# Retention by heads in a two-layer decoder step: half units of weights, 32-row state updates in four row groups

## What is computed

```python
RET_HEADS = 4; RET_QK_DIM = 256; RET_V_DIM = 512
q, k, v, g = jnp.split(x @ w_in, [hq, 2 * hq, 2 * hq + hv], axis=-1)    # w_in: 1024 x 6144
q, k = rope(q, pos), rope(k, pos) * RET_QK_DIM ** -0.5
inner = jnp.einsum('bihd,bjhd->bhij', q, k) * dmask[None]
o = jnp.einsum('bhij,bjhv->bihv', inner, v) + \
    jnp.einsum('bihd,bhdv->bihv', q, state) * cross_decay[None, :, :, None]
new_state = chunk_decay[None, :, None, None] * state + \
    jnp.einsum('bjhd,bjhv->bhdv', k * k_decay[None, :, :, None], v)
on = ((of - mu) * lax.rsqrt(var + LN_EPS)) * gain
return (jax.nn.silu(g) * on) @ w_out                                    # w_out: 2048 x 1024
```

## Time and profile before

| what | value |
|---|---|
| time, median of 3 runs (lowest to highest) | 1177.4 us (1176.07 to 1180.37) |
| profiled execution, span | 1174.3 us, mean granted clock 0.974 |
| TensorE products busy | 1087.4 us, 93% |
| VectorE busy | 569.8 us, 49% |
| ScalarE busy | 329.5 us, 28% |
| DMA | 319.72 MB, mean 272 GB/s |
| retention with its output products | 548.3 to 896 us |
| experts of layer 1 | 896 to 1174.3 us |
| share of the chain that ended last | TensorE 76%, DMA 9%, VectorE 9% |

### The profile page before, as it was taken

One profiled execution on the slowest core, in us unless ns is written; L12 is line 12 of the kernel. 1 busy time (PEld: TensorE's weight loads), 2 busy tenths in 40 slices (PEclk: granted clock), 3 DMA queues, 4 the chain that ended last, 5 costly groups with the idle time before them and its releaser, 6 DMA issues.

```text
span 1174.3 us, 14472 instructions
## 1 busy us (share of the span) xinstructions
PE 1087.4 (93%) x5486; PEld 638.7 (54%) x5486; DVE 569.8 (49%) x1080; ACT 329.5 (28%) x532; POOL 42.6 (4%) x77
## 2 busy tenths in 40 slices
PE   6999988999999899988999999999799899998991
PEld 5877655645443434335888765456687443434330
DVE  3877585636232223229684336658547323232325
ACT  4335256404111111113444213326413211111110
POOL 1300000000000000000000001111000000000000
PEclk9999999989999999999999999999898999999996
DMA  9434381946599999991433468996538699999951
GB/s 315 123 122 155 115 318 55 380 172 258 213 428 428 429 428 428 412 370 43 143 126 117 145 222 306 355 338 254 176 147 323 250 429 428 428 429 428 411 201 45
DMA packets 62842, 319.72 MB, mean 272 GB/s; under 512 B 4978, under 2 KB 5010, under 8 KB 50370
## 3 DMA queue, kind: packets, MB, share of 16 engines
q1 hardware_dynamic: 54338, 288.93, 62.2%
q0 software_dynamic: 8160, 28.80, 6.6%
q10 hardware_dynamic: 288, 1.23, 0.3%
HBM read 296.05 MB, written 22.89 MB: 272 GB/s over the span
## 4 chain that ended last, share of the span: by engine, by line
PE 76%; DMA 9%; DVE 9%; ACT 2%; issue 2%; SPq 1%; DVEq 0%; POOL 0%; ACTq 0%; POOLq 0%
PE bank L1147 27%; PE bank L979 17%; PE bank L1008 7%; DMA ring<-in_w_exp_up 7%; PE bank L946 3%; PE bank L1436 3%; PE bank L1212 2%; DMA ring<-in_w_in_attn 1%; PE bank L958 1%; PE bank L1426 1%; PE bank L959 1%; PE bank L1451 1%; PE bank L1308 1%; PE bank L1344 1%; PE bank L1330 1%
## 5 line engine op out<-in xcount | busy, mean ns | idle before, releaser
L1147 PE MATMUL bank<-ring_parts,XTt_parts 128*128 128x512 f32 x576 | 182.7, 398 | 4.0 <-DVE ring_parts L2153 2.8
L1147 PE MATMUL bank<-ring_parts 128*128 128x512 f32 x576 | 181.4, 393 | 0.0
L979 PE MATMUL bank<-ring,XTt 128*64 128x512 f32 x768 | 169.5, 598 | 11.8 <-DMA ring<-in_w_exp_up 9.9
L1147 PEld LDWEIGHTS bank<-ring_parts,XTt_parts 128*128 128x128 f32 x576 | 107.2, 190 | 33.2 <-issue 10.9
L979 PEld LDWEIGHTS bank<-ring,XTt 128*64 128x64 f32 x768 | 56.9, 138 | 121.3 <-issue 105.5
L1147 PEld LDWEIGHTS bank<-ring_parts 128*128 128x128 f32 x576 | 107.9, 189 | 24.4 <-issue 1.8
L1976 DVE TENSOR_TENSOR arena<-XTt,bank 128x512 f32<-128x512 f32 x16 | 17.2, 1073 | 208.9 <-PE bank L979 208.9
L1008 PE MATMUL bank<-ring,arena 128*64 128x512 f32 x512 | 115.1, 602 | 0.0
L694 DVE TENSOR_TENSOR ring_parts<-ring,ring_parts 128x4096 fp32r<-128x4096 f32 x22 | 97.1, 4419 | 33.6 <-ACT ring_parts L689 33.6
L689 ACT ACTIVATE ring_parts<-ring 128x4096 fp32r<-128x4096 f32 (+1 forms) x26 | 83.6, 3224 | 15.3 <-DMA ring<-in_w_in_attn 7.1
L1600 ACT ACTIVATE arena<-bank 128x512 f32<-128x512 f32 (+6 forms) x116 | 53.5, 489 | 93.6 <-PE bank L1147 48.9
(11 more groups left out here) (258 smaller groups left out, 1267.3 us busy)
## 6 DMA issues: line engine op xcount, KB each, us to landing
ring<-in_w_exp_down SPq DMA_DIRECT2D x32, 2048.0 KB, 13.4
ring<-in_w_exp_up SPq DMA_DIRECT2D x32, 2048.0 KB, 16.5
ring<-in_w_exp_gate SPq DMA_DIRECT2D x16, 2048.0 KB, 12.2
arena<-in_w_exp_gate SPq DMA_DIRECT2D x16, 2048.0 KB, 18.1
ring<-in_w_in_ret SPq DMA_DIRECT2D x12, 2048.0 KB, 9.0
ring<-in_state_ret SPq DMA_DIRECT2D x16, 1024.0 KB, 6.6
out_state_s<-ring POOLq DMA_DIRECT2D x16, 1024.0 KB, 6.3
ring<-in_w_in_attn SPq DMA_DIRECT2D x6, 2048.0 KB, 8.2
```

The costliest lines, as they stand in the source:

```text
L979: last = pe.matmul(ps[64 * j:64 * j + 64, :], xs[:, k, x0:x0 + 64], w[:, k, :], start=(k == 0), stop=(k == KC - 1))
L1147: last = pe.matmul(ps[:, 0:width], x(t, a, k), w[c][:, k, 0:width], **at)
```

## The change

Retention is written anew as six rounds. Round p has the units 2p and 2p + 1 of a new order of `w_in`: unit 2h is q and k of head h side by side (256 columns of each), unit 2h + 1 its v, units 8 to 11 the gates. In rounds 1 to 4 TensorE makes, between the tiles of these units, all of head p - 1: scores, the sample's outputs from its states, the prompt's state and outputs, and the updates of the head's sample states. Every unit is loaded, copied, split and multiplied in two halves of four lines (1 MB): raw halves in slots 0 and 5, copies in slot 4. The head's sample states are four pieces (two sequences each, 1 MB) in slots 1 and 2; each is updated, stored, and reloaded with the next head's. An update is four products of 32 rows. The roped tiles of q and k alternate between the two buffers of `RR` in all rounds; ScalarE copies the keys out (`keys_of`) and applies the prompt's key decay, which was VectorE's (L2387). The sample's moments go with the prompt's, head by head. The output units 0 to 3 get slots 1, 0, 5, 1 and copies in 2, 3, 4, 2. The order of the first expert loads is as it was.

The diff, cut to its core:

```diff
-          + [("rin", u) for u in range(8)] + [("state", 0), ("rin", 8), ("state", 1), ("rin", 9), ("state", 2)]
...
+          + [("retention", 0)] + [("rout", u) for u in range(4)]
...
-    for n, where, copy_at in ((0, 0, 2), (1, 1, 3), (2, 5, 4), (3, 0, 2)):
+    held[0], held[1], held[2] = ("rin", 10), ("pieces", 0), ("pieces", 1)
+    held[3] = held[4] = held[5] = ("rin", 11)
+    for n, where, copy_at in ((0, 1, 2), (1, 0, 3), (2, 5, 4), (3, 1, 2)):
...
+    def update(h, r):
+        for i in range(4):
+            take(("update", h, r, i), 4 + i)
...
+        def high_half(act, j):
+            act.wait_ge(half_in[j % 4], HALF_LANDED[j])
+            if j < 2:
+                wait_let_go(act, ("moe0", 3 * NE - 2))
+            else:
+                half_done(act, j - 2)
+            act.activation(unit_high()[:, half_lines(j)], unit_raw(j // 2)[:, half_lines(j)], ACT.Copy).then_inc(half_high, 1)
```

The loads, on the SP queue:

```diff
+            for p in range(5):
+                half(4 * p + 4)
+                half(4 * p + 5)
+                if 1 <= p < RH:
+                    piece(p, 0)
+                    piece(p, 1)
+                half(4 * p + 6)
+                if 1 <= p < RH:
+                    piece(p, 2)
+                half(4 * p + 7)
+                if 1 <= p < RH:
+                    piece(p, 3)
```

The update products and the order of a round, on TensorE:

```diff
+            def update(h, r):
+                if r == 0:
+                    pe.wait_ge(twice_ready, h + 1)
+                    pe.wait_ge(k_copied, 3 * h + 3)
+                pe.wait_ge(kd_ready, 4 * h + r + 1)
+                for i in range(4):
+                    ps, c, own = fill(("update", h, r, i)), i // 2, slice(32 * i, 32 * i + 32)
+                    pe.matmul(ps[:, :], kd[own, r % 2, c * 128:(c + 1) * 128], v[own, 2, h, :], start=True, stop=True)
...
+            for p in range(6):
+                a, b, h = 2 * p, 2 * p + 1, p - 1
+                works = 0 <= h < RH
+                if p == 0:
+                    first_half()
+                else:
+                    part_of(a, 0, 0)
+                    if works:
+                        scores_of(h)
+                    part_of(a, 0, 1)
+                    if works:
+                        sample_out(h)
+                        states_of(h)
+                    else:
+                        turn_o(a - 9, 0)
+                    part_of(a, 0, 2)
+                    if works:
+                        outputs_of(h)
+                part_of(a, 1, 0)
+                if works:
+                    update(h, 0)
+                elif p:
+                    turn_o(a - 9, 1)
+                part_of(a, 1, 1)
+                part_of(a, 1, 2)
+                if works:
+                    update(h, 1)
+                elif p:
+                    turn_o(a - 9, 2)
+                turn, n = (turn_qk, p) if p < RH else (turn_o, b - 9)
+                part_of(b, 0, 0)
+                part_of(b, 0, 1)
+                turn(n, 0)
+                if works:
+                    update(h, 2)
+                part_of(b, 0, 2)
+                part_of(b, 1, 0)
+                turn(n, 1)
+                part_of(b, 1, 1)
+                if works:
+                    update(h, 3)
+                part_of(b, 1, 2)
+                turn(n, 2)
```

Rope, sums and the order of rounds 0 to 3 and of the start of round 4, on VectorE:

```diff
+            def rope_qk(h, t):
+                k, r = 3 * h + t, ROWS[t]
+                if t == 2:
+                    fold(NIN + 2 * h + 1, ("rin", 2 * h, t), RE[:, k % 2, :])
...
+                if k >= 2:
+                    wait_full(dve, "rturn", (k - 2) // 3, (k - 2) % 3)
+                    dve.wait_ge(k_copied, k - 1)
+                rope(RE[:, k % 2, :], RR[:, k % 2, :], rropeA, table_r[:, t], 2, RQ, r, (re_used, k + 1), rk_ready)
...
+            def updated(h, r):
+                for i in range(4):
+                    ps = wait_full(dve, "update", h, r, i)
+                    st = pieces[r][:, i % 2, i // 2, :]
+                    dve.scalar_tensor_tensor(out=st, in0=st, scalar=GAMMA8[h], in1=ps[:, :],
+                                             op0=ALU.mult, op1=ALU.add).then_inc(freed(("update", h, r, i)), 1)
...
+                if p < RH:
+                    if works:
+                        scales(h)
+                    rope_qk(p, 0)
+                    if works:
+                        updated(h, 0)
+                        keys_for(h, 2)
+                    rope_qk(p, 1)
+                    rope_qk(p, 2)
+                    if works:
+                        updated(h, 1)
+                        keys_for(h, 3)
+                    low_half(dve, 2 * a + 3)
+                    if works:
+                        updated(h, 2)
+                    low_half(dve, 2 * a + 4)
+                    if works:
+                        updated(h, 3)
+                    fold(NIN + a + 2, ("rin", a + 1, 2), v[:, 2, p, :])
+                elif works:
+                    scales(h)
+                    gate(0, 0)
+                    updated(h, 0)
+                    keys_for(h, 2)
+                    gate(0, 1)
+                    half(0)
+                    updated(h, 1)
```

More of the change, by code:

```diff
@@ L100 @@
 PLACE, BEFORE, HIGH, HIGH_BEFORE = plan_slots()
[L101 removed]
+PARTED = [("in", u) for u in IN_ORDER] + [("rout", n) for n in range(4)]
 WIDE = 256 + 2 * SAMPLE
@@ L644, in wait_let_go @@
         def wait_let_go(eng, key):
-            if key and key[0] == "state":
-                for half in range(2):
-                    eng.wait_ge(state_stored[key[1]][half], 16)
+            if key and key[0] == "pieces":
+                for r in (2 * key[1], 2 * key[1] + 1):
+                    eng.wait_ge(piece_stored[r], 32 * RH)
             elif key and key[0] == "rout" and key[1] % 2 == 0:
@@ new lines, in first_half @@
+            def first_half():
+                pe.wait_ge(half_high, 1)
+                for t in range(3):
+                    wait_emptied(pe, "x2", t, 0)
+                    wait_emptied(pe, "x2", t, 1)
+                    project(fill(("rin", 0, t)), t, x_parts, unit_parts(0), stop=False, of=(0,), ks=range(4))
+                pe.wait_ge(half_low, 1)
+                for t in range(3):
+                    last = project(bank[t], t, x_parts, unit_parts(0), start=False, stop=False, of=(1,), ks=range(4))
+                last.then_inc(half_used, 1)
@@ L1465, in turn_o, with turn_qk @@
+            def turn_qk(h, t):
+                k, r = 3 * h + t, ROWS[t]
+                pe.wait_ge(rk_ready, k + 1)
+                ps = fill(("rturn", h, t))
+                for c in range(4):
+                    last = pe.transpose(ps[:, c * 128:c * 128 + r], RR[0:r, k % 2, c * 128:(c + 1) * 128], ident[0:r, 0:r])
+                last.then_inc(full(("rturn", h, t)), 1)
             def turn_o(n, t):
@@ new lines, in sample_out @@
+            def sample_out(h):
+                wait_emptied(pe, "sinner", h)
+                wait_emptied(pe, "rin", 2 * h + 1, 2)
+                pe.wait_ge(qm_ready, h + 1)
+                ps = fill(("so", h))
+                for g in range(2):
+                    pe.matmul(ps[32 * g:32 * g + 32, :], innS[0:64, 32 * g:32 * g + 32], v[0:64, 2, h, :], start=True, stop=False)
+                for r in range(4):
+                    pe.wait_ge(piece_in[r], 32 * (h + 1))
+                    for c in range(2):
+                        for g in range(2):
+                            at = 64 * c + 32 * g
+                            last = pe.matmul(ps[at:at + 32, :], QM[:, c, 4 * g + r, :], pieces[r][:, g, c, :],
+                                             start=(c == 1 and r == 0), stop=(r == 3))
+                last.then_inc(full(("so", h)), 1)
@@ L2416, in state @@
-            def state(s):
-                st = weights(("state", s))
-                for j in range(8):
-                    h, c, _ = update_of(j)
-                    ps = wait_full(dve, "update", s, j)
-                    dve.scalar_tensor_tensor(out=st[:, 2 * h + c, :], in0=st[:, 2 * h + c, :], scalar=GAMMA8[h], in1=ps[:, :],
-                                             op0=ALU.mult, op1=ALU.add).then_inc(freed(("update", s, j)), 1)
-                if s < NSEQ - 1:
-                    keys_of(s + 1)
```

793 lines of the change are left out of this document (406 added, 387 removed).

## The result

The changed kernel took 1225.5 us (median of 4 runs, 1214.95 to 1235.03) beside 1176.8 us for the kernel before, measured with it: ratio 1.0365, interval 1.0316 to 1.0414. It is slower by 48.7 us, where 16.7 were forecast. Run again later it took 1213.5 us (6 runs, 1210.35 to 1230.79), ratio 1.0273 (1.021 to 1.0335). The profiled execution (1214.95 us) has a span of 1213.3 us.

What follows compares the result with a forecast made beforehand. TensorE's work bounds retention; TensorE and DMA rings together bound the second mixture of experts. Retention: -21.2 - 8.1 + 5.4 + 32.9 = +9.0 us; expert loads +7.7; sum +16.7, so 1194 us, range 1179 to 1208.

Steps and rivals of the forecast that it cites:

- work without the waits: TensorE in retention: 21.2 us less for updates, 8.1 less for old waits and their clock, 5.4 more for smaller pieces.
- turn buffer and update 2, three times: Rounds 1 to 3: VectorE's rope waits for tile 0's turn, so update 1's sums hold update 2; 5.0 us each, 15.0.
- update 1, rounds 1 to 3: Update 0's sums stand behind other VectorE work, so the last bank is late by 0.8 us each round; 2.4.
- update 1, round 4: Update 0's sums stand behind the first gate's normalizations, table load and Silu; TensorE waits 2.8 us.
- state pieces, three times: TensorE waits for the fourth state piece's store and reload; 1 us each, 3.0 in all, ends 0 and 3 each.
- lower clock after waits: TensorE at 1.2 GHz after five waits in retention, 1.4 us lost each; 7.0 us, ends 0 and 10.
- expert loads: Behind retention: four loads wait for the last output product, 19.6 us, less an 11.9 us DMA pause they fill; 7.7 later.
- The update at 1.05 us: Retention: an update's 8 instructions over four row groups and four banks take 1.05 us; sixteen take 16.8, 21.2 less.
- Rival C: Row groups in updates do not run side by side: 1207.8 us two at a time, 1216 if held by emptying; chance 0.08.
- Rival A: VectorE keeps up at the turn of tile 0, rounds 1 to 3, so sums are ready: 1172.5 us; chance 0.12.
- Rival B: Behind retention, the expert loads catch up, so the 7.7 us go: 1186.3 us; chance 0.12.
- D: Small retention waits (2.4, 2.8, 3.0 us) and half the clock losses are hidden: 1182.3 us; chance 0.13.

Runs made afterwards that it cites:

- Experiment 11: Changed kernel plus five order edits: update 1's sums before tile 2's rope, expert loads, prompt's states first, first gate later, fourth piece before half unit; 1159.3 us, ratio 0.9787.
- experiment 1: Changed kernel with VectorE making update 1's sums and the next low half ahead of the rope of tile 2; 1188.4 us, ratio 1.0011 to the kernel before.
- experiment 5: Changed kernel with the fourth state piece ahead of the last half unit on the load queue; 1201.5 us, ratio 1.0174 to the kernel before.
- Experiment 3: Changed kernel with the prompt's state products ahead of the sample's outputs on TensorE; 1197.6 us, ratio 1.0157 to the kernel before.
- experiment 2: Changed kernel with the first expert loads ordered 0, 3, 5, 4, 1, 2 for the new slots; 1210.9 us, ratio 1.0252 to the kernel before.

## Why the prediction was right and wrong

The direction was right, and so were the places of all waits. The size was not: 1194 forecast, 1225.5 measured. Experiment 11 has the changed kernel's work on TensorE in 258.9 us with no idle time, 1.2 of them the stalls that are left at update 1. So 257.7 us are work, and that splits the 31.6 us of the stage:

| term | forecast | measured |
|---|---|---|
| work without the waits (257.7 - 279.6) | -23.9 | -21.9 |
| turn buffer and update 2, three times | 15.0 | 17.5 |
| low half in round 0 | 2.7 | 2.8 |
| update 1, rounds 1 to 3 | 2.4 | 1.1 |
| update 1, round 4 | 2.8 | 2.3 |
| state pieces, three times | 3.0 | 13.2 |
| lower clock after waits | 7.0 | 16.6 |
| stage | 9.0 | 31.6 |
| expert loads | 7.7 | 8.5 |

Measured waits are idle time plus what an update takes over 1.07 us: 3 x (3.21 + 2.63) at the turns, 0.37 each at update 1 (1.44 long), 0.65 + 1.68 in round 4. (The 6.1 of the text above count from 0.35 after the turn's start, where the next instruction begins elsewhere; idle time counts from the turn's end at 0.60.) The clock's term is what is left: 311.2 - 257.7 - 36.9. An estimate from the other side agrees: of the 44.4 us at 0.50, some 32 lie outside the idle times and the stalled updates, and half of them is 16.

- *The update at 1.05 us*: right, 1.07 (605.37 to 606.44), in each of the nine updates that nothing held; with two row groups 1.92, forecast 1.9. Rival C is out. The Trainium skill, TensorEngine Tiling (Array Packing), "PSUM Bottleneck", which says that the emptying may be what bounds a tiled product, held for the seven updates at which VectorE was late: 3.70 us at update 2 behind the turn, 1.44 at update 1, 2.75 in round 4. Where VectorE was on time, projection covered the emptying of 2.48 us.
- *VectorE held at the turn*: right, with the place and nearly the size. Rival A's condition, VectorE ahead, is what experiment 1 made.
- *The state pieces' round trip, "I take 1 us, three times"*: **the step that failed.** It was given ends of 0 and 3 us; the waits were 3.87, 4.46 and 4.89. The sum had the store at the 6.3 us of the earlier trace rows and the load at 4.9, "shorter alone", with nothing added for what is in flight beside them, though the code puts a half unit's load and the third piece's there; the queue's order was at hand in the diff. The load was 4.9 us from its issue to the product, as forecast, but it could be issued only 9.9, 10.5 and 10.8 us after the first store was. Where the half unit fell beside the load instead (experiment 1), the store was short, 6.2 us, and the load long, 8.7, and the round trip was the same. 2.0 us of a wait were the half unit's on average (experiment 5). The Trainium skill, SBUF — State Buffer, "The DMA setup-cost knee (why "@ 1 MiB" ≠ asymptote)", gives 2 us plus the bytes at 436 GB/s for a transfer, 4.4 us for 1 MB. An estimate from that page for store and load is 8.8. The trace's load of 1 MB with nothing beside it took 4.9, near the page's figure; its 15.1 for both is of rings with other transfers in them, and decides.
- *The lower clock, 1.4 us a wait*: **the other step that failed**, beyond its upper end of 10 us. I took the price from one short dip and counted five losses of 1.4 us, none for the pieces; here seven stretches of 3.4 to 10.2 us came with seven waits, 44.4 us in all, of which part lies in the waits themselves, and cost 2.4 us each. Experiment 3 (11.4 of idle time gone, 19.5 of the stage) and experiment 1 (12.9 of idle time and 7.9 within updates gone, 30.4 of the stage) show the clock going with the wait.
- *The work on TensorE*: 2.0 too favourable; where in the smaller pieces is not measured.
- *The loads*: right in cause (experiment 2) and size (8.5; 7.1 in the repeat). The reasoning with the pause was wrong in form. The late loads did not fill the pause, it moved ahead of them; and the gate's weights, put in the range only, were late by 5.07. Rival B is out, D too.
- *From span to median*: 9.1 us of the miss are no term of the sum. The median lay 12.2 above the profiled span in the first measurement, whose four executions include the 1232.8 and the 1235.0, and 2.4 in the repeat; 3.1 were carried over. The four parts are 22.6 in the stage, 0.8 behind, -1.2 at the start and 9.1 here, 31.3 of 31.5.

## What to carry to other kernels

When a buffer's reuse makes an engine wait, look at what stands behind that wait in its queue and who waits for it: here an order of a few lines was worth 30 us, and five edits of order took the change from 3 to 4% slower to 2% faster with its work untouched. Cost a store that must land before a reload by what is in flight beside it, and put what is wanted a round later behind it on the queue. After slots are renumbered, check each order of loads written out by hand. Look at the granted clock after a wait of TensorE: the waits of this stage, stalled updates in, were 36.9 us and cost 16.6 more, not quite half as much again. That is a sum over a stage and no price for one wait: behind the stage a wait of 3.30 us had a stretch of 3.4 at 0.50 (1109.1) and one of 3.27 had none (1049 to 1056 at 1.00).

## What was not expected of the hardware

- With idle times of 2.8 to 4.9 us on TensorE came 3.4 to 10.2 us at a granted clock of 0.50, beginning late in the wait or up to 1.6 us after it, though other products followed at once. At the same wait of 3.21 us and an update of 3.70 us the stretch was 10.2 us twice with 32-row updates, 6.8 in a third execution of the same retention, and 3.4 with 64-row ones.
- Of products of 32 rows over four row groups and four banks, 8 took 1.07 us; as many over 64 rows in two row groups took 1.92.
- A store and reload of 1 MB took 15.1 to 16.1 us beside two other loads, whichever of the two they lengthened; with one of them behind it, 12.9 in two of three rounds (last sum at 634.22 to TensorE at 647.13) and 15.0 in the third.
